# A two-layer diffusion backbone on one core: the first head's work among the last modulation quarters, five output products among the last heads

## The reference, cut to what matters

```
m = silu(cond) @ mod_w[l] + mod_b[l]                 # 6 vectors: shift, scale, gate, twice
h = rms_norm(x) * (1 + scale1) + shift1
# layer 1:
z = h @ od_w_in                                      # Fourier part, q latent, kv latent, k_pe
q = rms_norm(qc) @ od_w_uq                           # 12 heads of 64 + 32
k, v = split(rms_norm(kvc) @ od_w_ukv)               # 12 heads of 64 and 64
p = softmax(scale * (q_nope k_nope^T + q_pe k_pe^T)) # per head; latent rows read 384 keys
out = concat(fourier, p @ v) @ od_w_out              # 1024 x 1024
x = x + gate1 * out
x = x + gate2 * hier_moe(rms_norm(x) * (1 + scale2) + shift2)
```

## Time and profile before

| | us |
|---|---|
| median of 3 timed runs | 755.17 (753.98 to 755.49) |
| span of the profiled execution, first to last instruction | 748.4 |
| TensorE busy, matmuls | 685.6 |
| VectorE busy | 246.5 |
| GpSimd busy | 165.4 |
| ScalarE busy | 142.0 |

### The profile page before, as it was taken

The page is one execution under the profiler, slowest core; times in us unless marked ns, Lnnn a source line. Parts: engine busy times, 40 slices in busy tenths (PEclk is TensorE's granted clock), DMA queues, the critical chain, the costliest instruction groups (busy, mean ns, idle before and its releaser), DMA issues.

```text
span 748.4 us, 9564 instructions
## 1 busy us (share of the span) xinstructions
PE 685.6 (92%) x3667; PEld 387.9 (52%) x3667; DVE 246.5 (33%) x525; ACT 142.0 (19%) x291; POOL 165.4 (22%) x221
## 2 busy tenths in 40 slices
PE   1799999999999999899989999899899999999990
PEld 0344444564565666556444454356445566666650
DVE  0200312211237223223551423555312733232346
ACT  2100100000221212112132110555112122121201
POOL 5000111011331122212111100357223122222202
PEclk9899999999989999999999999999999899999996
DMA  9999999299539999998580685904501969989842
GB/s 336 394 363 345 381 410 388 82 404 424 244 143 394 407 423 421 420 422 351 198 324 2 249 332 186 376 2 184 183 1 41 409 269 417 421 358 421 332 174 100
DMA packets 53207, 219.46 MB, mean 293 GB/s; under 512 B 13773, under 2 KB 20941, under 8 KB 33968
## 3 DMA queue, kind: packets, MB, share of 16 engines
q1 hardware_dynamic: 31520, 178.59, 59.7%
q0 software_dynamic: 9664, 23.41, 8.3%
q10 hardware_dynamic: 11984, 16.92, 6.5%
HBM read 206.53 MB, written 20.68 MB: 304 GB/s over the span
## 4 chain that ended last, share of the span: by engine, by line
PE 73%; DMA 16%; DVE 6%; issue 2%; ACT 2%; POOL 0%; SPq 0%; ACTq 0%; POOLq 0%; DVEq 0%
PE ps L1396 13%; PE ps L1310 11%; PE ps L1468 7%; PE ps L1421 6%; DMA pool<-in_mod_w 5%; PE ps L1504 5%; PE ps L1245 4%; DMA pool<-in_moe_w 4%; DMA pool<-h_rows,of_now 4%; PE ps L1455 3%; PE ps L1485 3%; PE ps L1638 3%; PE ps L1563 2%; PE ps L1298 2%; PE ps L1383 2%
## 5 line engine op out<-in xcount | busy, mean ns | idle before, releaser
L1396 PE MATMUL ps<-pool 128*64 128x256 f32 x928 | 103.6, 379 | 2.2 <-issue 2.1
L1396 PEld LDWEIGHTS ps<-pool 128*64 128x64 f32 x928 | 76.5, 137 | 31.5 <-issue 9.5
L1310 PE MATMUL ps<-pool,turned 128*128 128x512 f32 x192 | 84.6, 595 | 0.0
L1245 PE MATMUL ps<-pool,cs 128*32 128x512 f32 x384 | 48.3, 630 | 18.5 <-DMA pool<-in_mod_w 9.7
L1468 PE MATMUL ps<-turned,pool 128*128 128x384 f32 x192 | 65.1, 492 | 0.0
L1310 PEld LDWEIGHTS ps<-pool,turned 128*128 128x128 f32 x192 | 35.7, 190 | 41.3 <-issue 41.1
L1421 PE MATMUL ps<-pool 128*64 128x512 f32 x240 | 54.8, 597 | 1.9 <-DMA pool<-in_moe_w 0.8
L1468 PEld LDWEIGHTS ps<-turned,pool 128*128 128x128 f32 x192 | 36.8, 196 | 30.9 <-issue 8.9
L964 DVE SCALAR_TENSOR_TENSOR pool<-ps,pool 128x256 f32<-128x256 f32 x20 | 9.7, 484 | 113.0 <-PE ps L1396 113.0
L417 POOL TENSOR_SCALAR rstd<-ss 128x1 f32<-128x1 f32 x24 | 10.6, 441 | 160.1 <-ACT xn L583 119.6
L547 POOL TENSOR_SCALAR pool<-pool 128x384 f32<-128x384 f32 (+1 forms) x30 | 30.5, 1031 | 59.3 <-DVE pool L1159 59.2
(11 more groups left out here) (245 smaller groups left out, 899.7 us busy)
## 6 DMA issues: line engine op xcount, KB each, us to landing
pool<-in_moe_w SPq DMA_DIRECT2D x72, 1024.0 KB, 15.1
pool<-in_mod_w SPq DMA_DIRECT2D x24, 2048.0 KB, 12.6
turned<-in_moe_w SPq DMA_DIRECT2D x18, 1024.0 KB, 14.4
pool<-in_ev_w_in SPq DMA_DIRECT2D x6, 1024.0 KB, 20.0
y_rows<-pool ACTq DMA_DIRECT2D x8, 768.0 KB, 20.2
xn<-in_moe_w SPq DMA_DIRECT2D x6, 1024.0 KB
pool<-y_rows ACTq DMA_DIRECT2D x12, 512.0 KB, 6.6
pool<-in_ev_w_in SPq DMA_DIRECT2D x2, 2048.0 KB, 23.1
```

The lines of the kernel that those rows point to most:

```text
L1245: ins = mm(ps[32 * j:32 * j + 32, 7, :], cs32[:, 2 * part + c, :], w[:, c, j * 512:(j + 1) * 512], start=part + c == 0, stop=part + c == 4)
L1310: ins = mm(ps[:, 2 * t + n, :], yT[:, k, t * P:(t + 1) * P], weight(parts[k // 4], 4, D)[:, k % 4, n * 512:n * 512 + 512], start=k == 0, s ...
L1396: ins = mm(ps[m, k, 0:DE], hTe.rearrange("p (c n) -> p c n", c=DC)[:, cc, m], w[e][:, cc, :], start=cc == 0, stop=cc == DC - 1)
```

## The change

In TensorE's program keys and query transposes of head 0 stand ahead of the modulation quarters of third (1, 2), the scores of head 0 between quarters 1 and 2, the query transposes of head 1 between quarters 2 and 3. These quarters write bank 5 and not bank 7. The wait for the modulation rows stands in head 1's turn. In the last turn and behind it, five of the eight products of the first output block (tile 0, half 0, k = 0 to 4) are done by `first_out`; `project_out` begins that block at k = 5. In VectorE's program the modulation rows stand behind the maxima of head 0 and the query copy of head 1.

```diff
-            def mod_rows(l, i):
+            def mod_rows(l, i, bank=7):
                 dve.wait_ge(*L(3 * l + i, "mod_mm", 4))
...
-                    link(v_.tensor_tensor(mrow[l][:, i, :], ps[:, 7, :], mrow[l][:, i, :], ALU.add))
+                    link(v_.tensor_tensor(mrow[l][:, i, :], ps[:, bank, :], mrow[l][:, i, :], ALU.add))
...
-            mod_rows(1, 2)
             head_q(0)
+            head_maxima(0)
             head_q(1)
-            head_maxima(0)
+            mod_rows(1, 2, bank=5)
...
-            def mod_part(l, i, part):
+            def mod_part(l, i, part, bank=7):
...
-                        ins = mm(ps[32 * j:32 * j + 32, 7, :], cs32[:, 2 * part + c, :], w[:, c, j * 512:(j + 1) * 512],
+                        ins = mm(ps[32 * j:32 * j + 32, bank, :], cs32[:, 2 * part + c, :], w[:, c, j * 512:(j + 1) * 512],
...
-            def project_out(l, parts, last):
+            def first_out(ks):
+
+                for k in ks:
+                    mm(ps[:, 0, :], yT[:, k, 0:P], weight(f"out1.{k // 4}", 4, D)[:, k % 4, 0:512], start=k == 0, stop=False)
+
+            def project_out(l, parts, last, begun=0):
...
-                        for k in range(DC):
+                        for k in range(begun if (t, n) == (0, 0) else 0, DC):
...
-            pe.wait_ge(S("vv"), 3)
-            for part in range(4):
-                mod_part(1, 2, part)
-            pe.wait_ge(S("q_rot"), 1)
-            pe.wait_ge(S("q_out"), 3)
-            pe.wait_ge(S("vv"), 4)
-            pe.wait_ge(S("kpeT"), 1)
...
+            pe.wait_ge(S("q_out"), 3)
+            pe.wait_ge(S("kpeT"), 1)
             k_pair(0)
+            pe.wait_ge(S("q_rot"), 1)
             head_q(0)
+            mod_part(1, 2, 0, bank=5)
+            mod_part(1, 2, 1, bank=5)
+            pe.wait_ge(S("vv"), 4)
             head_scores(0)
+            mod_part(1, 2, 2, bank=5)
             head_q(1)
-            pe.wait_ge(S("mod_row"), 6)
+            mod_part(1, 2, 3, bank=5)
             for h in range(NH):
                 if h + 1 < NH:
                     head_scores(h + 1)
+                if h == 1:
+                    pe.wait_ge(S("mod_row"), 6)
                 if h % 2 == 0 and h + 2 < NH:
                     k_pair(h // 2 + 1)
                 if h + 2 < NH:
                     head_q(h + 2)
+                if h == NH - 1:
+                    arrived(pe, "out1.0")
+                    arrived(pe, "out1.1")
+                    pe.wait_ge(S("qT"), NH)
+                    first_out((0,))
                 if h > 1 and h % 2:
                     pair_values(h // 2 - 1)
+                if h == NH - 1:
+                    first_out((1,))
                 if h:
                     head_probs(h - 1)
+            first_out((2, 3))
             head_probs(NH - 1)
+            first_out((4,))
             pair_values(NH // 2 - 1)
-            arrived(pe, "out1.0")
-            arrived(pe, "out1.1")
-            project_out(1, ("out1.0", "out1.1"), (S("o_out"), NH // 2))
+            project_out(1, ("out1.0", "out1.1"), (S("o_out"), NH // 2), begun=5)
```

More of the change, by code:

```diff
@@ L760, in mod_rows @@
                 if i < 2:
-                    v_.tensor_tensor(mrow[l][:, i, :], ps[:, 7, :], mrow[l][:, i, :], ALU.add).then_inc(S("mod_row"), 1)
+                    v_.tensor_tensor(mrow[l][:, i, :], ps[:, bank, :], mrow[l][:, i, :], ALU.add).then_inc(S("mod_row"), 1)
                 else:
-                    link(v_.tensor_tensor(mrow[l][:, i, :], ps[:, 7, :], mrow[l][:, i, :], ALU.add))
+                    link(v_.tensor_tensor(mrow[l][:, i, :], ps[:, bank, :], mrow[l][:, i, :], ALU.add))
                     dve.wait_ge(S("gain_rows"), 32 * (l + 1))
```

## The result

Timed beside the kernel before, the changed kernel took 747.96 us (median of 8 runs, 743.03 to 749.83) against 754.0 (8 runs, 750.94 to 756.92): ratio 0.9916, 95% interval 0.9888 to 0.9944, so 6.3 us less by the ratio. A second timing of the same kernel gave 746.99 (6 runs) and 0.9907 (0.987 to 0.9944). The forecast was 749.4 with a range of 748.0 to 751.5: the direction and the two places were right, the gain of 5.8 was close, and the median lies 0.04 us under the lower end. That distance is far inside the noise; the second timing lies 1.0 us under it.

What follows compares the result with a forecast made beforehand. TensorE, busy in 92% of the span, was taken as the bound. Gains of 2.0 us at the front and 3.8 at the tail sum to 5.8, taking the timed 755.17 to 749.4 us, range 748.0 to 751.5.

Steps and rivals of the forecast that it cites:

- The standstills before scores 0 and 1: TensorE's waits for key and query copies at heads 0 and 1, 0.94 and 0.73 us, were to go.
- all covers: Copies and loads at the first heads were to finish before TensorE needs them; 0.2 us left before scores 2.
- The front: Modulation, first keys, queries and scores: reordering them was to gain 2.0 us, bounds 1.1 and 2.2.
- I take 0.05 for each of four: Cost in us of each new seam between unlike products among the modulation quarters, chosen between nothing and 0.27.
- The tail: Last heads and first output block: five products moved into idle pieces were to gain 3.8 us, bounds 3.0 and 4.4.
- The step-by-step play: Last heads replayed in old time with five products inserted: first output block ends at 535.2 for 539.15, gain 3.95 us.
- the idle sum: Four TensorE idle pieces before pair 4, heads 10 and 11 and pair 5: 3.84 us, taken as the most winnable.
- the last step: Whole kernel: 5.8 us gain set against the timed median 755.17, keeping its 6.8 us distance above the span: 749.4.
- +-1.2 us at most: Routing stage: how far a shifted fall of the clock from 2.4 to 1.2 GHz could move the time.
- the front's gain is eaten: Rival: copy waits return in a later head because of VectorE's modulation rows; only 3.8 us remain, 751.4; chance 0.08.
- Products standing in the way: Rival: in-order output products delay head 11's softmax chain, losing 1.8 of the 3.8 us, 751.2; chance 0.08.
- The slower case: Rival: in the expert rounds gathered token rows land later beside shifted loads, 756.7 us and up; chance 0.03.

Runs made afterwards that it cites:

- repeat of before: The kernel before, nothing changed, profiled three more times: 755.17, 754.13 and 753.72 us.
- the fourth quarter in the wait: Changed kernel with the fourth modulation quarter behind head 2's query transposes, and VectorE's modulation rows behind head 2's query copy: ratio 0.9945 to the kernel before.
- all in one place: Changed kernel with all five early output products between the transposes of heads 10 and 11: one execution, 747.29 us.
- the front alone: Changed kernel without the early output products, so only the reordered modulation, keys, queries and scores: ratio 1.0002 to the kernel before.
- the tail alone: Kernel before with only the five early output products, modulation and first head as before: ratio 0.9936 to the kernel before.
- the idle fillers: Kernel before plus five never-read filler products where the changed kernel has its early output products: ratio 1.0001 to the kernel before.
- the widest piece filled: Kernel before plus two filler products in the 1.65 us idle piece ahead of head 11's transposes only: one execution, 751.64 us.
- the run with fewer changes: Changed kernel with modulation quarter 2 moved ahead of the scores of head 0: ratio 0.9936 to the kernel before.

## Why the prediction was right or wrong

**Right.** Both places, and what was to happen in each. The standstills before scores 0 and 1 went, the one before scores 2 stayed at 0.8 (the query copy of head 2 ended 0.2 us ahead of the key copy, the cover that I had worked out), the middle heads carried the shift unchanged, all covers held: with the later loads of output weights (first issue 467.05, that is 4.25 us behind the first keys' start, where the earlier trace rows has 1.92 behind the front's start) nothing on TensorE waited for a transfer in this stretch. The stages from the first output block to the first expert round took 61.18 against 61.19 us.

**The front was over-sized: 2.0 taken, 1.27 measured.** The failed term is "I take 0.05 for each of four" seams. The order was costed at 14.48 us from first to second keys; it took 478.19 - 462.80 = 15.39. The 0.91 between them is 0.27 in the modulation (3.57 + 1.85 + 1.85 against 7.00), 0.25 in two groups of query transposes (0.46 + 0.47 against 0.68) and 0.40 in two groups of scores (3.42 against 3.02). I had named 0.27 per seam as the bound from the nearest row and then gone to the other end without a row for it. My bound for how much earlier scores 2 start, 1.7 to 2.2 us, was missed.

**The tail was under-sized: 3.8 taken, 4.19 measured.** The step-by-step play gave 3.95, and I cut it to the idle sum with "more can hardly be won". More was won: I had costed the transposes of heads 10 and 11 at 1.0 each, and in the chain they take 0.76 and 0.77. They are not shorter themselves (0.93 in the timeline after, 0.98 and 0.95 in the earlier trace rows); with a product right behind them their last 0.2 us lies under its start. That gives 0.47, of which product 1 (1.05 for 0.9) and the three products behind the shift (2.77 for 2.65) take 0.27 back. The five products took 4.49 us in the gaps against the 4.41 that I had for them in a row, which I had named as a sign of being wrong; it is 0.08. The errors of front and tail nearly cancel, 5.8 forecast and 5.47 in the profile, and that is luck.

**What put the median outside the range** is the last step: I set the gain against 755.17 and gave 0.7 us for the spread of the runs. The base was mis-sized: three runs within 1.5 us did not show the spread, eight runs of before reach from 750.94 to 756.92, and their median is 754.0. With the forecast's own 5.8 from there, it would have been 748.2. The interval of the first timing is 2.1 us to each side, where I had 1.5 as the least that can be told from no change. (The lower bound of both parts together, given as 4.2, is 1.1 + 3.0 = 4.1; nothing hangs on it.) A second misreading did not move the number: a run takes 1.9 us more than its span, in each profile where both are given (748.79 and 746.9 after; 755.17 and 753.3 in a repeat of before). So the execution with span 748.4 took about 750.3, worked out from that 1.9, and was a quick one; I read the distance of 6.8 as a constant, which it isn't.

**And one term was put at nothing.** The profiled execution of before happened to keep its clock through the tail, so its idle pieces seemed to cost 3.84 us and nothing else. In two of four executions of the kernel before they cost 1.4 and 1.5 us more. Half of 1.5 on top of 5.47 is 6.2, and the two timings give 6.3 and 7.0 (0.9916 of 754.0, 0.9907 of 754.15), with 2 to 3 us on either side. That the clock falls there in some executions, and its price, is shown; that this makes up the difference is an estimate (754.0 less 6.2 is 747.8, against 747.96), and the timings can't tell it from chance. I had looked for the clock only in the routing stage, and my "+-1.2 us at most" for it was too small as well: that stage took between 59.96 and 63.99 us.

The Trainium skill's 215.7 ns, which the prediction names and sets aside, stand in TensorE: Matmul & The Clock Gate, section Step-by-step: what each phase is for; section Back-to-back issue gap, which I named, gives about 216.

**The rivals.** That the front's gain is eaten did not happen by VectorE, but the fourth quarter in the wait shows how near it was: 1.4 us of modulation rows one step later cost 0.65. Products standing in the way are real where they exceed the standstill (2.35 us with all in one place), but spread as they are they cost 0.1. The slower case, gathers that take longer, looked true at first. The pages give for the transposes of gathered rows, over both layers, the idle time of the matmuls before them and the part that a gather ended (last two numbers), after and before:

```profile
L1388 PE MATMUL ps<-cst,pool 128*128 128x128 f32 x176 | 28.7, 288 | 5.7 <-DMA pool<-h_rows,of_now 4.3
L1383 PE MATMUL ps<-cst,pool 128*128 128x128 f32 x176 | 28.7, 287 | 2.8 <-DMA pool<-h_rows,of_now 1.4
```

But 1.9 against 0.9 of it lie in layer 0, which runs ahead of every change. In layer 1 it is 2.5 against 0.5; the second execution of the same changed kernel has 0.4, and the three repeats of before have 0.7, 2.0 and 1.4. The rounds of layer 1 took 149.9 and 149.5 in the changed kernel and 148.1, 149.1, 148.6 and 148.9 in that of before. The means differ by 1.0 us, but other kernels spread as widely without the whole change: 148.3 with the front alone, 148.2 with the tail alone, 147.3 and 148.6 with the idle fillers, 149.5 with the widest piece filled. Two executions can't settle whether the change adds anything there. By one of the prediction's own signs (the stretch from the first output block to the end grew, by 1.8) it would have been wrong; one execution of each could not carry that sign. The 2.2 us ahead of the change are no effect of it either: the third repeat of before reached that point at 462.8.

## What to carry to other kernels

Work that stands behind the last wait of a stage and has its inputs early is worth nearly its full length (here 4.19 of 4.41 us) if it is cut up to fit the standstills ahead of it; put in one piece it pays only for one of them (1.84). A standstill on one engine isn't free if the work put there releases a second engine's work ahead of what the first engine waits for next. Weigh a gain against several timed runs and stage lengths, not against one span: here one span moved by 1.5 us while the changed stretch moved by 5.5.

## What the runs showed of the hardware that I had not expected

TensorE's clock fell to 1.2 GHz behind idle pieces of 0.7, 0.8 and 1.65 us, none of them long, with small products between (busy 2.15 of 5 us), and only in some executions of the same kernel: three of five, with the same busy time where it stayed up. It cost 1.4 to 1.5 us each time, since it was down for some 3 us of dense work.

The same fall in the routing stage, which every execution has, came in different lengths and so set the time by itself. Where the clock was down for 6.8 us, in eleven of fourteen executions, the stage from first output block to first expert round took 61.16 to 61.56 us. It was down for 13.7 us in the first repeat of before (63.95) and with the quarter in the wait (63.99), and for 3.4 us with the products in one place (59.96). No instruction differs there between these kernels.

A change between unlike matmuls costs 0.1 to 0.2 us even when nothing is waited for: 0.13 for entering products that write 32 rows each, 0.13 on the transposes ahead of them, 0.20 on the scores behind them. One of each of the first two fell away in the run with fewer changes; the third is read from rows only.
